# First ring unit issued when the input rows have landed, squares ahead of exp and tanh on ScalarE, and 24 constant products at the head of TensorE's program

## The reference

```python
def rmsnorm(x, g):
    xf = x.astype(jnp.float32)
    y = xf * lax.rsqrt(jnp.mean(xf * xf, axis=-1, keepdims=True) + EPS)
    return (y * g.astype(jnp.float32)).astype(x.dtype)
...
def mixer_rglru_fox(h, w_in, conv_w, conv_b, w_a, b_a, w_i, b_i, lam, b_f, w_out):
    z = h @ w_in
    u, gate, q, k, v, f_logit = jnp.split(z, [...], axis=-1)
    y_a = rg_lru(causal_depthwise_conv(u, conv_w, conv_b), w_a, b_a, w_i, b_i, lam) * jax.nn.gelu(gate)
    log_f = jax.nn.log_sigmoid(f_logit.astype(jnp.float32) + b_f.astype(jnp.float32))
    y_b = forgetting_attention(q.reshape(shp), k.reshape(shp), v.reshape(shp), log_f).reshape(bsz, s, FOX_W)
    return jnp.concatenate([y_a, y_b], axis=-1) @ w_out
```

## Time and profile before

| | |
|---|---|
| median of 3 runs | 1770.99 us (1769.68 to 1776.07) |
| the profiled execution's own time | 1769.93 us |
| its span, first to last instruction | 1768.1 us |
| busy: TensorE, VectorE, ScalarE | 1539.0, 617.0, 257.1 us |
| mean granted TensorE clock | 0.934 of full speed |
| read from HBM | 391.31 MB, 223 GB/s over the span |

### The profile page before, as it was taken

How to read it: one execution, slowest core, us unless ns; L and a number is a source line. 1 busy time by engine, 2 the same in 40 slices (tenths; PEclk the granted TensorE clock), 3 DMA queues, 4 the chain that set the end, 5 groups by cost and what they waited for, 6 DMA issues and landing times.

```text
span 1768.1 us, 20858 instructions
## 1 busy us (share of the span) xinstructions
PE 1539.0 (87%) x8992; PEld 1158.1 (66%) x8992; DVE 617.0 (35%) x1327; ACT 257.1 (15%) x606; POOL 30.3 (2%) x52
## 2 busy tenths in 40 slices
PE   6999999999999999999999999989977665576665
PEld 4868888888876788888887788768853222121211
DVE  3726215357533441253576637632230000000000
ACT  1322021000011510210001222222021000000000
POOL 0000000000010000000000012000000000000000
PEclk9999999999999999999999899998979988867878
DMA  9334416665443054157644002332739999999997
GB/s 377 140 118 157 177 48 235 241 231 205 172 143 143 1 191 162 41 226 280 259 176 165 14 1 97 118 96 97 324 125 428 430 428 429 430 428 430 428 428 326
DMA packets 42827, 395.27 MB, mean 224 GB/s; under 512 B 15856, under 2 KB 18288, under 8 KB 19056
## 3 DMA queue, kind: packets, MB, share of 16 engines
q1 hardware_dynamic: 42032, 392.46, 56.0%
q0 software_dynamic: 272, 1.05, 0.2%
q10 hardware_dynamic: 432, 0.44, 0.1%
HBM read 391.31 MB, written 2.62 MB: 223 GB/s over the span
## 4 chain that ended last, share of the span: by engine, by line
PE 74%; DMA 23%; DVE 2%; issue 1%; ACT 1%; ACTq 0%; DVEq 0%
PE pb L449 51%; DMA ring<-in_w_experts 22%; PE pb L869 11%; PE pb L538 6%; PE pb L810 3%; DMA small_w<-in_small_w 1%; PE pb L599 1%; PE pb L659 0%; ACT arena L1348 0%; PE pb L1174 0%; DVE rstd L1704 0%; PE pb L1181 0%; PE pb L882 0%; PE pb L1034 0%; DVE xT L2399 0%
## 5 line engine op out<-in xcount | busy, mean ns | idle before, releaser
L449 PE MATMUL pb<-hT,ring 128*128 128x256 f32 x2176 | 483.5, 382 | 0.0
L449 PEld LDWEIGHTS pb<-hT,ring 128*128 128x128 f32 x2176 | 412.7, 191 | 62.1 <-issue 6.9
L2387 DVE SCALAR_TENSOR_TENSOR side<-side,pb 128x256 f32<-128x256 f32 x16 | 6.7, 421 | 410.6 <-ACT side L1348 410.6
L1348 ACT ACTIVATE arena<-pb 128x512 f32<-128x512 f32 (+4 forms) x162 | 74.8, 472 | 511.0 <-PE pb L449 393.5
L449 PE MATMUL pb<-ring,hT 128*32 128x512 f32 (+2 forms) x512 | 93.5, 652 | 39.9 <-DMA ring<-in_w_experts 39.4
L449 PE MATMUL pb<-arena 128*64 128x128 f32 (+5 forms) x592 | 95.0, 445 | 28.0 <-DMA arena<-in_w_experts 15.9
L538 PE MATMUL pb<-arena,ring 128*128 128x256 f32 x512 | 118.2, 382 | 0.0
L449 PE MATMUL pb<-ring,arena 128*32 128x512 f32 (+1 forms) x416 | 68.1, 764 | 46.4 <-DMA ring<-in_w_experts 46.4
L538 PEld LDWEIGHTS pb<-arena,ring 128*128 128x128 f32 x512 | 94.9, 190 | 14.6 <-issue 2.9
L449 PEld LDWEIGHTS pb<-arena 128*64 128x64 f32 (+3 forms) x592 | 55.5, 165 | 63.9 <-issue 26.9
L449 PEld LDWEIGHTS pb<-ring,hT 128*32 128x32 f32 (+1 forms) x512 | 32.7, 142 | 89.3 <-DMA ring<-in_w_experts 49.0
(11 more groups left out here) (325 smaller groups left out, 1707.9 us busy)
## 6 DMA issues: line engine op xcount, KB each, us to landing
ring<-in_w_dense SPq DMA_DIRECT2D x86, 2048.0 KB, 7.9
ring<-in_w_experts SPq DMA_DIRECT2D x72, 2048.0 KB, 36.2
arena<-in_w_experts SPq DMA_DIRECT2D x24, 2048.0 KB, 36.1
ring<-in_w_dense SPq DMA_DIRECT2D x2, 1536.0 KB, 6.7
cons<-in_cons SPq DMA_DIRECT2D x1, 1808.0 KB, 19.6
xT<-in_xT SPq DMA_DIRECT2D x1, 1024.0 KB, 6.3
side<-in_memT POOLq DMA_DIRECT2D x1, 1024.0 KB, 6.2
out<-xT SPq DMA_DIRECT2D x4, 256.0 KB, 2.2
```

The costliest lines, as they stand in the source:

```text
L449: return nc.tensor.matmul(o, l, r, start=st, stop=sp)
L1348: return nc.scalar.activation(o, i, f, **kw)
L2387: V.scalar_tensor_tensor(tg[:, e % 2, :], tg[:, e % 2, :], 1.0, ps[:, 0:S], ALU.add, ALU.mult).then_inc(eg_ready, 1)
```

## The change

SP waits for xT before it issues ring unit 0. `small_w` gets a semaphore of its own, `small_w_in`, waited for ahead of `ab_f` only; the other waits for small loads go to 32, the first two. ScalarE runs a square root of one column first, then the squares and the norm's root, and only then the exp and the tanh of the parameters. VectorE writes `epsm` first and signals it (`filler_ready`), and its silu and softplus chain moves behind the norm's eight chunks. TensorE multiplies `epsm` by itself 24 times into a part of bank 3 that nothing reads, ahead of its first wait for loads.

```diff
--- before.py
+++ after.py
@@ -311,6 +311,7 @@
         loaded = [sem(f"slot_loaded{i}") for i in range(SLOTS + 2)]
         filled = [sem(f"bank_filled{i}") for i in range(8)]
         freed = [sem(f"bank_freed{i}") for i in range(8)]
+        small_w_in, filler_ready = sem("small_weights_loaded"), sem("filler_rows")
         small_in, late_in, lru_w_in = sem("small_loaded"), sem("constants_loaded"), sem("lru_w_loaded")
         x_in, mem_in, out_sent = sem("x_loaded"), sem("mem_loaded"), sem("out_sent")
         hs_ready = sem("h_scaled")
@@ -748,9 +749,13 @@
                             mark(last, f"sum{q}")
 
 
-            pe.wait_ge(small_in, 48)
+            pe.wait_ge(filler_ready, 1)
+            for i in range(24):
+                nc.tensor.matmul(pb[:, 3, 0:P], epsm, epsm, start=True, stop=True)
+            pe.wait_ge(small_in, 32)
             norm("ab")
             ready = chunk_wait(h_ready)
+            pe.wait_ge(small_w_in, 16)
             ps = fill("ab_f")
             for k in range(DC):
                 ready(k)
@@ -1264,6 +1269,7 @@
                     sp.dma_start(T64[rows_of(b), :, rows_of(b % 2)], row_blocks((inv_d, invT_d)[b // 2], b // 2, b)).then_inc(t64_in, 16)
 
             sp.dma_start(xT, a["xT"].rearrange("(c p) t -> p c t", p=P)).then_inc(x_in, 16)
+            sp.wait_ge(x_in, 16)
             for u in range(len(units)):
                 w, nr, ncol = units[u]
                 t, at = slot_at(slot_of[u])
@@ -1455,16 +1461,16 @@
 
             act.dma_start(cons[:, 0:EARLY], a["cons"][:, 0:EARLY]).then_inc(small_in, 16)
             act.dma_start(cols[:, :], a["cols"]).then_inc(small_in, 16)
-            act.dma_start(small_w[:, :], a["small_w"]).then_inc(small_in, 16)
-            act.wait_ge(small_in, 48)
+            act.dma_start(small_w[:, :], a["small_w"]).then_inc(small_w_in, 16)
+            act.wait_ge(filler_ready, 1)
+            fn(warm, epsm[:, 0:1], ACT.Sqrt)
+            act.wait_ge(x_in, 16)
+            squares(xT)
+            act.wait_ge(small_in, 32)
+            root("ab")
             act.wait_ge(sp_abs, 1)
             fn(sp_t[1], sp_t[0], ACT.Exp, scale=-1.0).then_inc(sp_exp, 1)
             fn(csil, col("c", 0, 8), ACT.Tanh, scale=0.5).then_inc(c_tanh, 1)
-
-
-            act.wait_ge(x_in, 16)
-            squares(xT)
-            root("ab")
             act.wait_ge(pads, 1)
             for i in range(2):
                 copy(f"ab_u{i}", up[:, 2 * i:2 * i + 2, 3:3 + S], pairs)
@@ -1810,23 +1816,22 @@
             masked = [0]
 
 
-            dve.wait_ge(small_in, 48)
+            V.memset(epsm, EPS).then_inc(filler_ready, 1)
+            dve.wait_ge(small_in, 32)
             link(V.tensor_scalar(sp_t[3], col("lam", 0, 4), -1.0, None, ALU.mult))
             V.scalar_tensor_tensor(sp_t[0], sp_t[3], -1.0, sp_t[3], ALU.mult, ALU.max).then_inc(sp_abs, 1)
             V.memset(eps2, EPS * EPS)
-            V.memset(epsm, EPS)
             V.memset(up[:, :, 0:3], 0.0).then_inc(pads, 1)
             V.tensor_scalar(hba, col("b_a", 0, 4), 0.5, None, ALU.mult)
             V.tensor_scalar(hbi, col("b_i", 0, 4), 0.5, None, ALU.mult).then_inc(hb_ready, 1)
             V.tensor_scalar(wq8, col("q_norm"), 0.125, None, ALU.mult)
+            norm("ab", lambda c: col("ab_norm", c))
             dve.wait_ge(c_tanh, 1)
             link(V.scalar_tensor_tensor(csil, csil, 1.0, col("c", 0, 8), ALU.add, ALU.mult))
             V.tensor_scalar(csil, csil, 0.5, None, ALU.mult).then_inc(c_ready, 1)
             log1p(sp_t, 1, c4, sp_t[3])
             link(V.tensor_scalar(c4, c4, 4.0, None, ALU.mult))
 
-
-            norm("ab", lambda c: col("ab_norm", c))
 
             ps, free = full(dve, "ab_f")
             V.tensor_scalar(fz[3], ps[0:8, 0:S], col("fox_b")[0:8, :], -1.0, ALU.add, ALU.mult).then_inc(free, 1)
```

## The result

The changed kernel's median is 1754.94 us (5 runs, 1754.64 to 1760.22), that of the kernel before 1770.99 (5 runs, 1769.51 to 1779.5). The ratio is 0.9897, 95% interval 0.988 to 0.9915: faster by 1.0%, and outside the range that I gave.

A forecast was written before the change was run, and what follows sets the result against it. TensorE was taken to set the pace up to the experts, whose groups then wait for weights. A start gain of 8.1 us, carried whole, made 1769.9 into 1761.8, or 1762.9 for a median; range 1759 to 1767.

The forecast's parts named there:

- I therefore carry the gain whole: From the first ring matmul to the end: the 8.1 us gained at the start reaches the kernel's end undiminished.
- Step 6: SP's hold of ring unit 0 until x lands: cost zero, cover 4.7 us, and no gain for x.
- Step 4: 24 products at TensorE's head: low clock for about 5.5 us, end at 9.1, so they, not x, start the norm.
- the second rival: Low-clock stretches fall elsewhere later, 1766 to 1768, 14%; its cited rule: cold matmuls vary by run, so no single fillers value.
- Step 5: Norm 3.6 us, pause 2.93, `ab_f` 5.0: first ring matmul at 20.6 instead of 28.7, a gain of 8.1 us.
- my two bounds: `ab_f` takes 3.7 us if the clock holds through the pause, 6.8 if it is low throughout.
- Steps 2 and 3: Exp and tanh behind the root, VectorE's small chain behind row chunks ending at about 18.9: nothing waits, no cost.
- Step 1: `small_w`'s own semaphore, exp and tanh behind the root: alone moves the norm's start from 14.40 to 7.6.
- The sum: Whole kernel: 1769.9 - 8.1 = 1761.8 for the profiled execution; its median, 1.1 above, 1762.9.
- The rivals: Kinder clock (20%), low stretches elsewhere (14%), change does nothing, 1770 to 1771 (3%), slower through low clock into ring units (3%).
- The clock is kinder: Fillers reach full clock sooner or the pause before `ab_f` keeps it: gain 9.3 to 10.9, 1760.1 to 1761.7, 20%.
- low stretches elsewhere: In the 1,300 us behind the start, two or three more low-clock stretches leave a gain of 3 to 5, 14%.

The follow-up runs named there:

- experiment 3: The changed kernel without the hold: ring unit 0 issued at once instead of after xT lands; 1763.57 us, ratio 0.9945 to the kernel before.
- the repeat: The changed kernel itself measured once more, beside other versions on one chip; 1753.65 us, ratio 0.9888 to the kernel before.
- experiment 2: The kernel before with only `epsm` written first and the 24 products added at TensorE's head; 1768.78 us, ratio 0.9978.
- (5): The changed kernel with 40 products of 32x32 more behind the norm, 256 instructions added in all; 1759.1 us, ratio 0.9918 to the kernel before.
- experiment 7: The changed kernel with its 24 products cut to 32x32, the same 96 instructions; 1754.12 us, ratio 0.9886 to the kernel before.
- experiment 10: The changed kernel with its 24 products cut to 32x32, measured a second time; 1756.58 us, ratio 0.9907 to the kernel before.
- experiment 12: The changed kernel with 16 products at the head instead of 24, and 12 in the pause behind the norm; 1756.2 us, ratio 0.9902 to the kernel before.

## Why the prediction was wrong, point by point

The forecast was 1762.9 and the median 1754.94, 8.0 us below. Of these 1.0 are the start, 3.9 the pauses and the clock near 1190, 0.5 small differences along the way, and 2.5 where the two profiled executions stand among their kernels' times. The step that failed by most is "I therefore carry the gain whole". Step 6's zero is wrong too, but has no share in this pair of traces.

- **Step 4, the fillers.** Mis-sized. I let them stay low for 5.5 us, as the norm of before had; they changed to the full pace near 4.0, after 3 us, and ended at 7.9, not 9.1. Right was that they, and not x, start the norm. Worth 1.2 us. But no single value would have been right: in the other traces with the same 24 products at the head the change came after 3.2 us (experiment 3), 4.2 (the repeat), 5.6 (2) and 5.8 (5), as the second rival had said of this step.
- **Step 5, norm, root, rows.** Right: 3.6, 3.0 and 5.1 us. With step 4 the first ring matmul stood at 19.6, predicted 20.6; a gain of 9.1, not 8.1. In the repeat it stood at 20.43, so how near 20.6 came is in part luck of the execution. The clock fell in the pause before `ab_f` here and in the repeat. Behind a pause as long (3.03 us) `ab_f` took 6.5 us in experiment 7 and 3.6 in experiment 10, which are one kernel; that is near my two bounds.
- **Steps 2 and 3.** Right: nothing waited for exp, tanh or the small chain. Step 3's 18.9 for the end of the row chunks counted the first chunk twice; by its own rows it was 18.4, and nothing hung on it.
- **Step 1, the split.** Right where it was predicted. Its size rested on one execution in which the small loads had been served early.
- **Step 6, the hold.** Wrong, though not seen in the two profiled executions, which both were of the good kind. Its sentence on x was right, and it stopped there. "small_w ... landed at 11.88 even with the ring's packets beside it" took one landing as the landing. In experiments 2 and 3 it was 17.6 and 17.8, and in 3 cols landed at 12.3. Taking the hold out of the changed kernel costs 8.5 us by the ratios (0.9945 against 0.9897), putting it alone into before gives 9.2. The rule that I weighed there (issue early, wait late; the Trainium skill, "DMA: Bandwidth & Descriptors", Rules for kernel authors) points the wrong way here, and I found it harmless for a reason that did not reach far enough. The same page of the Trainium skill, Queues, rings and completion order, has the rule that would have told: each engine turns between the queues that have work, packet by packet. The packets' counts agree with it (24 of cols beside 24 to 26 of the ring's in each microsecond), small ones passing in turn with the ring's.
- **"I therefore carry the gain whole."** The step that failed by most. It put everything behind 28.73 at nothing, and the fillers' 96 instructions are work for the instruction queue too. The 3.9 us near 1190 are 2.3 in the dense group (2.30 of pauses, of which 0.13 stay) and 1.6 of clock. The row of before that showed it was in the chain I read ("issue" 1.79 at 1191.07), and I passed it over as far from the edit.
- **The sum.** 9.1 at the start and 3.9 near 1190, with 0.5 of small differences, make the 13.5 between the two profiled spans. The medians are 16.0 apart. The other 2.5 are before's profiled execution standing 1.1 below its median, as I had carried over, and the changed kernel's standing 1.5 above its own, where I had assumed the same 1.1 below. No run gives a cause for these 2.5; I take them for scatter from execution to execution.
- **The rivals.** None of them was it. "The clock is kinder" held in step 4 only; low stretches elsewhere do move times: between experiment 12 and the repeat they took back 2.5 us of a lead of 2.7 at the start.

## What to carry to other kernels

Work out for every transfer on the path whose packets it shares the engines with: a wait behind the rows that are wanted first can protect the small loads more than the rows. If a pause in the chain is marked "issue" near dense small instructions, look at the times of the packets of the instruction queue, and take any edit that adds or removes instructions ahead of it as one that can move the pause. A single profiled execution says nothing of a landing's spread; of before's first three times two were within 1.4 us of one another and the third 5 us above, which hinted that there was one.

## What the runs showed that I had not expected

- Landings of the small loads have two kinds. In the trace of before cons, cols and small_w took 2.7, 5.5 and 10.2 us; in experiment 2, 4.1, 10.9 and 15.8. With the hold the third took 5.4 to 6.1 us in every trace, whichever the first took. The packets' times tell the kinds apart in all fourteen traces. In five (before and the changed kernel among them) the first packet of cons starts at 1.8 us and x's first at 2.0 to 2.3; in the other nine x's starts at 1.8 and cons' at 3.1. In the second kind without the hold (experiments 2 and 3) cols' first packet comes only at 6.2 and 5.9, behind the ring's first at 5.6 and 5.3; in before it came at 4.8, ahead of the ring's. What decides which queue is served first was not settled: both first issues start within 0.01 us of each other in all the traces. The issue of cols took 0.45 us in the first kind and 0.6 in the second. Before's times look like the two kinds too, among the last 11 six of 1769.2 to 1771.4 us and five of 1774.5 to 1779.6; that these are the kinds is not shown.
- The supply of instructions can bind: TensorE came to the end of a packet's 256 instructions and went on 1.2 to 1.6 us behind the next packet's landing. 24 products in idle time at the start took two pauses away 1,180 us later, and 40 more brought one back.
- Filling a pause with 12 products (2.84 us) kept the clock at its higher level and made `ab_f` 3.6 us instead of 5.1, in both kernels that had them; the whole did not become faster.
